# Fifteen quads of weight blocks by Strassen's seven products in a two-layer encoder trunk

## What is computed

```python
for layer in range(DEPTH):              # DEPTH = 2
    h = rms_norm(x, norm_w[layer])
    if layer % 2 == 0:
        z = h @ w_in_ab[e]              # 4096 x 13312
        ...                             # 16 + 16 heads
        x = x + y @ w_out_ab[e]         # 4096 x 4096
    else:
        z = h @ w_in_c[o]               # 4096 x 10240
        ...                             # 32 heads
        x = x + (oc * jax.nn.silu(gate)) @ w_out_c[o]
return rms_norm(x, final_norm_w)
```

## Time and profile before

| | us |
|---|---|
| median of 3 runs (2814.21 to 2814.45) | 2814.39 |
| the profiled execution | 2814.37 |
| its span, first to last instruction | 2812.6 |
| PE busy (12681 matmuls) | 2797.6 |
| PE loading stationary tiles | 2329.4 |
| DVE busy | 1687.7 |
| ACT busy | 1347.7 |
| DMA queue of the loads, share of 16 engines | 67.7% |

### The profile page before, as it was taken

How to read it: one execution, slowest core, us unless ns; L and a number is a source line. 1 busy time by engine, 2 the same in 40 slices (tenths; PEclk the granted TensorE clock), 3 DMA queues, 4 the chain that set the end, 5 groups by cost and what they waited for, 6 DMA issues and landing times.

```text
span 2812.6 us, 37759 instructions
## 1 busy us (share of the span) xinstructions
PE 2797.6 (99%) x12681; PEld 2329.4 (83%) x12681; DVE 1687.7 (60%) x2103; ACT 1347.7 (48%) x1654; POOL 16.4 (1%) x14
## 2 busy tenths in 40 slices
PE   9999999999999999999999999999999999999998
PEld 7888888888888888888888888888888888888886
DVE  7766666556556555566665556666655666665554
...
PEclk9999999999999999999999999999999999999999
...
GB/s 334 222 210 232 225 226 221 224 217 228 234 209 215 228 220 239 189 254 254 253 240 222 223 211 218 231 233 220 221 226 204 231 227 225 216 251 218 215 209 187
DMA packets 357923, 637.17 MB, mean 227 GB/s; under 512 B 25376, under 2 KB 79136, under 8 KB 357792
## 3 DMA queue, kind: packets, MB, share of 16 engines
q1 hardware_dynamic: 343824, 593.52, 67.7%
...
...
## 4 chain that ended last, share of the span: by engine, by line
PE 99%; DMA 0%; issue 0%; DVE 0%; ACT 0%; POOLq 0%; POOL 0%; SPq 0%; DVEq 0%; ACTq 0%
PE proj L1098 32%; PE proj L1099 32%; PE proj L1100 32%; PE o_ps L1099 1%; PE o_ps L1098 1%; PE sc_ps L1100 1%; PE o_ps L1100 1%; PE sc_ps L1099 1%; PE sc_ps L1098 1%; DMA raw<-in_w_in_ab 0%; DVE w_lo L757 0%; DVE x_fin L1091 0%; ACT w_hi L637 0%; POOLq L268 0%; POOL rms L598 0%
## 5 line engine op out<-in xcount | busy, mean ns | idle before, releaser
L757 DVE TENSOR_TENSOR w_lo<-raw,w_hi 128x1024 fp32r<-128x1024 f32 x990 | 1208.5, 1221 | 856.7 <-ACT w_hi L637 850.5
L637 ACT ACTIVATE w_hi<-raw 128x1024 fp32r<-128x1024 f32 x990 | 1049.6, 1060 | 1148.6 <-PE proj L1100 1087.3
L1098 PE MATMUL proj<-w_hi,h_hi 128*128 128x512 f32 x2936 | 1143.4, 389 | 2.0 <-issue 1.5
L1099 PE MATMUL proj<-w_lo,h_hi 128*128 128x512 f32 x2936 | 1142.8, 389 | 0.0
L1100 PE MATMUL proj<-w_hi,h_lo 128*128 128x512 f32 x2936 | 1142.1, 389 | 0.0
L1100 PEld LDWEIGHTS proj<-w_hi,h_lo 128*128 128x128 f32 x2936 | 551.2, 188 | 114.9
L1098 PEld LDWEIGHTS proj<-w_hi,h_hi 128*128 128x128 f32 x2936 | 551.4, 188 | 114.5 <-issue 2.4
L1099 PEld LDWEIGHTS proj<-w_lo,h_hi 128*128 128x128 f32 x2936 | 551.4, 188 | 109.9
L1098 PE MATMUL proj<-w_hi,y_hi 128*128 128x512 f32 x1024 | 398.4, 389 | 0.0
L1099 PE MATMUL proj<-w_lo,y_hi 128*128 128x512 f32 x1024 | 398.4, 389 | 0.0
L1100 PE MATMUL proj<-w_hi,y_lo 128*128 128x512 f32 x1024 | 398.3, 389 | 0.0
...
## 6 DMA issues: line engine op xcount, KB each, us to landing
...
raw<-in_w_out_ab SPq DMA_DIRECT2D x128, 512.0 KB, 4.5
raw<-in_w_out_c SPq DMA_DIRECT2D x128, 512.0 KB, 4.5
head_turn<-head_stage SPq DMA_DIRECT2D x256, 96.0 KB, 1.9
...
```

The lines of the kernel that those rows point to most:

```text
L637: nc.scalar.activation(w_hi[:, slot], raw[:, slot], ACT.Copy).then_inc(hi_ready, 1)
L757: nc.vector.tensor_tensor(w_lo[:, slot], raw[:, slot], w_hi[:, slot].bitcast(F32), ALU.subtract) \
L1098: nc.tensor.matmul(dst, hi, r_hi, start=start, stop=False)
L1099: nc.tensor.matmul(dst, hi, r_lo, start=False, stop=False)
```

## The change

Take the four blocks (0, c1), (1, c1), (1, c2), (0, c2) of a pair together: a 2 x 2 matrix of weight blocks, B11 and B12 from c1, B21 and B22 from c2, times the 2 x 2 matrix A of two token tiles by the two chunks. This is a **quad**. Instead of 8 products A(i,k) B(k,j) of 6 matmuls each it makes Strassen's seven (in Winograd's form), of sums and differences of the parts:

- left sums, made once per layer for a quad's c1, c2 (`make_sums`): S1 = A21 + A22, S2 = S1 - A11, S3 = A11 - A21, S4 = A12 - S2, split into high and low;
- right mixtures in each quad (`quad_lo`, DVE): B12 - B11, B22 - B12, B22 - (B12 - B11), B21 - that; then seven high parts (`quad_hi`, ACT) and seven low parts for seven products. Three go to spare tiles laid over unused rows, four to the ring;
- products go to the banks m1, m5, m6, m7 and three straight to `proj`; m1 and m6 are the two free banks, m5 lies on `sc_ps`, m7 on `o_ps`'s bank. A second quad of a pair adds on to them;
- once per pair, behind its last quad (at step q): at q+4 ACT copies m1 and DVE folds m6 and m7, at q+5 m5 twice, at q+6 into the banks of g = 0, and the drain of g = 0 is at q+7 or when the group is done; the folds into g = 1 stand at step 0 of the next pair (in the last pair before its late blocks).

Quads: one at blocks 12 to 15 in pairs 6, 8, 10, 14, 16, 28; two at 12 and 22 in pair 15, two at 6 and 16 in pairs 18, 23 and 29; one at 7 in pair 30. The sums are made in pair 6 (step 5), 14 (3 and 7), 17 (15 and 19) and 28 (3 and 7). The two-pair loop has two rounds, its third is written out; the loops over x1 pairs and the last x2 pairs are written out; two loops over qg pairs go from three rounds to two. The split of the k turn moves from step 5 to step 12. The core of the diff:

```diff
+QUAD = 4
+OPS = 8
+ONE_QUAD = with_quads([*REST1[:12], (2, 3), *REST1[12:]], REST1)
+TWO_QUADS = with_quads([*REST2[:6], (2, 3), *REST2[6:], (4, 5)], REST2)
+LATE_QUADS = with_quads([*REST2, (2, 3)], [*REST2[:6], (4, 5), *REST2[6:]])
...
-K_NORM_TURN, K_TURN = (0, 5, 7, 10), (0, 0, 2, 5)
+K_NORM_TURN, K_TURN = (0, 5, 7, 10), (0, 0, 2, 12)
...
-        (3, [Pair("in_ab", qk(1), "qk", "B", "vg", batch=4), Pair("in_ab", vg(1), "vg", "qk", "qk", v=2)]),
+        (2, [Pair("in_ab", qk(1), "qk", "B", "vg", batch=4),
+             Pair("in_ab", vg(1), "vg", "qk", "qk", v=2, quads=ONE_QUAD, heads=20, heads_step=4)]),
+        (1, [Pair("in_ab", qk(3), "qk", "B", "vg", batch=6)]),
+        (1, [Pair("in_ab", vg(3), "vg", "qk", "qk", v=4)]),
...
-        (3, [Pair("out_ab", out_cols(1), "x1", "h", "x1", x_batch=0)]),
+        (1, [Pair("out_ab", out_cols(1), "x1", "h", "x1", x_batch=0, quads=ONE_QUAD, heads=32,
+                  combine=((3, "x1", 0, 2), (7, "x1", 1, 4)))]),
...
+                    if b >= RING and p.quad_at(b - RING) is not None and p.quad_at(b - RING)[2] < 3:
+                        k, _, part = p.quad_at(b - RING)
+                        sp.wait_ge(mixed, QUAD * (p.quad_n + k) + part + 1)
+                    elif b >= RING:
+                        sp.wait_ge(lo_ready, p.o + p.freed[b - RING])
...
+                if part == 2:
+                    dve.wait_ge(mixed, mixes_done + 1)
+                    minus(mix3, b22, b12).then_inc(mixed, 1)
+                    lo(2, mix)
+                    dve.wait_ge(mixed, mixes_done + 2)
+                    dve.wait_ge(lo_ready, n + 3)
+                    minus(mix, b22, mix).then_inc(mixed, 1)
+                    lo(3, mix3)
...
+                if part == 0:
+                    times(0, of_tile(c1, 0), m1[:], opens, closes)
+                    times(1, of_sum(3), x12[:], opens, False)
+                if part == 1:
+                    times(2, of_sum(0), m5, opens, closes)
+                    times(3, of_sum(2), m7[:], opens, closes)
+                if part == 2:
+                    times(4, of_tile(c2, 0), x11[:], False, False)
+                    times(5, of_sum(1), m6[:], opens, closes)
+                if part == 3:
+                    times(6, of_tile(c2, 1), x21[:], False, False, 2)
```

More of the change, by code:

```diff
@@ L193, in plan @@
         n += rounds * len(pairs)
+        ops += rounds * pairs[0].o_step
+        quads += rounds * pairs[0].quad_step
+        folds += rounds * pairs[0].folds_step
         x += rounds * x_step
@@ L438, in turn_tiles, with folds_of, weights_of, scratch_of @@
             return za, (k_stage, q_stage)[k], (kT_hi, qT_hi)[k], (kT_lo, qT_lo)[k]
+        def folds_of(out):
+            one, two = {"vg": (zb, za), "qg": folds_c}.get(out, (parts_v, sums_v))
+            return one[:, 0], one[:, 1], two[:, 0], two[:, 1]
+        def weights_of(p, start, r):
+            if r % 2 == 0:
+                slot = (start + r // 2) % RING
+                return w_hi[:, slot], w_lo[:, slot]
+            return [tile[:] for tile in spare_of[p.spare][r // 2 % 2]]
+        def scratch_of(p):
+            parts, sums = (za, zb) if p.out in ("vg", "qg") else (parts_v, sums_v)
+            return parts[:].rearrange("p t (k n) -> p (t k) n", n=SEQ), \
+                sums[:].rearrange("p t (k j n) -> p (t k) j n", j=2, n=P)
         block = ctx.enter_context(nc.Block())
@@ new lines, in copy_m1, with sums_hi_at @@
+            def copy_m1(p, b):
+                if p.quads and b == p.last_quad + QUAD:
+                    act.wait_ge(folded, p.folds)
+                    act.wait_ge(block_done, p.o + p.op[p.last_quad] + OPS)
+                    nc.scalar.activation(folds_of(p.out)[0], m1[:], ACT.Copy).then_inc(m1_copied, 1)
+            def sums_hi_at(p, b):
+                for k, (at, stage, quad, _) in enumerate(p.combine):
+                    if b == at + 1:
+                        hi, _ = sums_of[stage][quad]
+                        act.wait_ge(sums_made, 4 * (p.combined + k + 1))
+                        _, sums = scratch_of(p)
+                        nc.scalar.activation(hi[:], sums, ACT.Copy).then_inc(sums_hi, 1)
@@ L643, in drain @@
+            def drain(p, g, out):
+                act.wait_ge(block_done, p.o + p.g0_done if g == 0 else p.o)
+                if g == 0 and p.quads:
+                    act.wait_ge(folded, p.folds + 6)
+                if g == 1 and p.after_quads:
+                    act.wait_ge(folded, p.folds)
                 for t in range(TT):
```

390 lines of the change are left out of this document (335 added, 55 removed).

## The result

The changed kernel takes **2795.76 us** in the median of 4 runs (2795.44 to 2796.74), beside 2814.3 us for the kernel before on the same chip: a ratio of 0.9935 (95% interval 0.9918 to 0.9953). The forecast was 2797.4 in a range of 2792.8 to 2805.5. The profiled execution took 2795.44 us, with a span of 2793.7; the span before was 2812.6, so 18.9 us are to be explained. A single run of 7282.65 us, among nine of the kernel with the folds together, is a slow one and left out of that kernel's range and ratio.

The account below looks back on a forecast made before the run. TensorE, busy 99% of the span, was taken to bound the kernel. From 2814.4 us, -20.4 (matmuls) - 0.9 (loop hole) + 3.0 + 1.0 + 0.3 (pairs 14, 28, 29) = -17.0 gave 2797.4 us, range 2792.8 to 2805.5.

Parts of the forecast that it names:

- -20.4 us for 90 matmuls: All 15 quads: each does 42 matmuls for 48, so 90 go at 0.2267 us each, -20.4 us.
- -0.9 for a loop's hole: Two-pair loop: two rounds for three leave one return, so one TensorE hole of 0.9 us goes.
- +3.0 in pair 14: Pair 14's quad: sums among the h turns make VectorE start it late; TensorE loses 3.0 us, bounds 0 and 4.8.
- 0.5 for a late third raw block: Pair 14's quad: the third raw weights' high part ends 0.5 us after VectorE could use it.
- +1.0 in pair 28: Pair 28's quad: high part 1 waits for the third raw block, low part 5 ends late; 1.0 us, bounds 0 and 2.
- I find leads of 2.3 us or more there: Folds and drain behind a quad: weights stay ready at least 2.3 us before TensorE wants them, so nothing is lost.
- (c): Rival, all quads: raw slots free late, the lead is lost, 3 to 4.8 us each, 2853 us; chance 0.05.
- +0.3 in pair 29: Pair 29's first quad, at block 6: third raw block lands in 3.9 us, low part 5 barely holds; 0.3 us.
- The sum: Whole kernel: the five terms, -20.4 - 0.9 + 3.0 + 1.0 + 0.3, make -17.0 us.
- (b): Rival, quads: ACT-DVE hand-overs cost 0.1 to 0.2 us more each, 7.5 us in all, 2805; chance 0.24 with small stalls.
- the slack of 1.4 us: Quads in the quiet state: low part 5 is ready 1.4 us before TensorE wants product 5, so nothing is lost.
- (d): Rival, pair 14: TensorE's clock falls to 1.2 GHz behind waits, a quad's matmuls cost 8.4 us more, 2806; chance 0.04.

## Why the prediction was right, and where not

- **-20.4 us for 90 matmuls** held: 12591 remain, twelve quads take 42 times 0.2267 us, and taking the quads out gives the time back (17.2 to 17.9 us for 17.5 by the steps). The 215.7 ns of the Trainium skill (TensorE: Matmul & The Clock Gate, "Wait — 56ns, not 53.3ns?") is not what this kernel's matmuls show, before or after.
- **-0.9 for a loop's hole** was too small: both went, -1.84. The step counted returns (two become one); the three runs without quads in the loop show that this count holds only there. Why a quad takes the hole away stays open.
- **+3.0 in pair 14** was the right place and mechanism, 2.13 in size. The row that the prediction laid out by hand was 0.3 us too late at its end, and its tenths for semaphores weren't there: product 5 begins 0.06 us after low part 5. Its 0.5 for a late third raw block was nothing in this trace (high part 1 begins at T-3.25, ahead of its want), but real in others: where that block took 5.6, 6.0 and 6.4 us to land, with pair 14 unchanged, the quad lost 2.6, 3.1 and 3.5 us. Moving the second sums takes the wait away, so the cause is shown.
- **+1.0 in pair 28** was the right size in the wrong place, and that its size came out is luck. Two steps failed. "The third raw block is issued at T-7.9": it was issued at T-9.2 (T-7.9 is the fourth's) and landed in 4.3 us for 4.9, so high part 1 ended at T-3.7 for T-1.9, low part 5 at T+5.86 for T+7.7, and the quad lost nothing. And "I find leads of 2.3 us or more there" for the folds. Behind the quad, a landing of 7.8 us with folds and drain after it lost 0.85 in this trace. The prediction had looked at landings before and in a quad, not at those asked for when low part 6 sets its slot free, though that wait of SP was named in rival (c).
- **+0.3 in pair 29** came out 0.61, by a third block that took 4.8 us to land and not 3.9; the text gave 1.1 for 5.4. Pair 16, counted at 0, lost 0.25.
- **The sum** of -17.0 stands beside -18.4 by the steps; the holes (-0.94) and pair 14 (-0.87) make most of the difference.
- **DVE** shows 1891 us and not 1905, **ACT** 1402 and not 1410: the quads' operations overlap in the records (starts 1.14 apart at 1.22 long), which the sum of durations doesn't know.
- Of the **rivals**, (b) is refuted as put: in the quietest quads low part 5 ends at T+5.24 for T+5.3, so the hand-overs add nothing. But the added operation shows how near it was: 1.1 us more of chain cost 10 to 12 us, since most quads have less than the slack of 1.4 us that the step gave to all. (c) didn't come: the load behind the fourth slot was late once, for 0.85 us. (d) didn't come in the changed kernel: the granted clock is 1.00 behind its waits in pairs 14 and 28, of up to 1.0 us. The run with the burst shows its mechanism, slow matmuls behind waits of 2.65 and 4.5 us.
- What the prediction undervalued was **the spreading of the folds and the drain**, which it took as costless. With it undone the change brings 7 us and not 18.5. It keeps a burst of 8 us away from a lead of 5.6.
